# Expert rows of a mixture-of-experts layer: the first one of a token written with its residual, the second added

## The reference

```python
gp = softmax(x @ w_group_router + b_group_router)        # x = rms_norm(h); 4 groups
g_val, g_idx = top_k(gp, 1)
el_sel = expert logits of that group                     # 8 experts each, 32 in all
e_val, e_idx = top_k(softmax(el_sel), 2)
gate = g_val * e_val / sum(e_val)
for e in range(32):
    hdn = silu(x @ w_gate[e]) * (x @ w_up[e])            # 1024 -> 256
    y = y + combine[:, e:e + 1] * (hdn @ w_down[e])      # 256 -> 1024
out = h + y
```

## Time and profile before

| | |
|---|---|
| median of 3 runs | 608.5 us (605.67 to 611.92) |
| the profiled execution | 608.44 us, of which its span is 606.7 us |
| TensorE busy | 536.3 us, 88% |
| DVE, ACT, GpSimd busy | 218.0, 168.9, 139.8 us |
| data moved by DMA | 140.97 MB, 232 GB/s over the span |
| links of the chain that are DMA | 36% of the span |

### The profile page before, as it was taken

How to read it: one execution, slowest core, us unless ns; L and a number is a source line. 1 busy time by engine, 2 the same in 40 slices (tenths; PEclk the granted TensorE clock), 3 DMA queues, 4 the chain that set the end, 5 groups by cost and what they waited for, 6 DMA issues and landing times.

```text
span 606.7 us, 9491 instructions
## 1 busy us (share of the span) xinstructions
PE 536.3 (88%) x3304; PEld 393.1 (65%) x3305; DVE 218.0 (36%) x602; ACT 168.9 (28%) x421; POOL 139.8 (23%) x230
## 2 busy tenths in 40 slices
PE   4899999999989999999978888878987699897794
PEld 4888988987557677788867545555644456554451
DVE  4754234333657755427772112202111112211111
ACT  6743343332434333125431201202111012111010
POOL 0232232222503300004535022222211222222212
PEclk9999999999989999999987999999998979998978
DMA  8741000012312111199979689999999999999993
GB/s 339 269 116 36 19 18 1 19 51 77 111 63 97 42 36 36 35 357 421 398 263 303 223 264 368 361 365 378 360 372 384 411 393 375 375 354 382 372 392 56
DMA packets 33458, 140.97 MB, mean 232 GB/s; under 512 B 10489, under 2 KB 11148, under 8 KB 21351
## 3 DMA queue, kind: packets, MB, share of 16 engines
q1 hardware_dynamic: 25776, 124.33, 53.6%
q0 software_dynamic: 5856, 12.60, 8.7%
q10 hardware_dynamic: 1766, 3.25, 1.4%
HBM read 131.15 MB, written 16.46 MB: 243 GB/s over the span
## 4 chain that ended last, share of the span: by engine, by line
DMA 36%; PE 16%; DVE 2%; issue 2%; ACT 1%; POOL 0%; SPq 0%; ACTq 0%; DVEq 0%; POOLq 0%
DMA expert_w<-in_w_gate 17%; DMA expert_w<-in_w_up 17%; PE ps L884 5%; PE ps L900 2%; DMA token_gates<-gate_rows 2%; PE ps L795 2%; PE ps L521 1%; PE ps L522 1%; PE ps L526 1%; PE ps L780 1%; PE ps L823 1%; PE ps L769 1%; PE ps L912 1%; POOL out L1708 0%; PE ps L871 0%
## 5 line engine op out<-in xcount | busy, mean ns | idle before, releaser
L884 PE MATMUL ps<-expert_w,xT 128*64 128x256 f32 x1120 | 128.5, 387 | 15.2 <-issue 5.6
L884 PEld LDWEIGHTS ps<-expert_w,xT 128*64 128x64 f32 x1120 | 93.7, 140 | 53.4 <-issue 23.5
L900 PE MATMUL ps<-expert_w,hT 128*64 128x512 f32 x272 | 66.6, 633 | 17.2 <-DVE hT L1546 16.0
L1702 POOL DMA_INDIRECT out<-y_sb,idx_now x17 | 27.2, 1597 | 161.2 <-issue 85.2
L1539 DVE SCALAR_TENSOR_TENSOR hid<-s_act,gate,ps 128x256 f32<-128x256 f32 x18 | 12.0, 665 | 140.1 <-ACT s_act L1171 140.1
L900 PEld LDWEIGHTS ps<-expert_w,hT 128*64 128x64 f32 x272 | 22.5, 145 | 50.7 <-issue 48.5
L1171 ACT ACTIVATE s_act<-ps,gate 128x256 f32<-128x256 f32 x18 | 8.5, 473 | 132.1 <-PE ps L884 132.1
L521 PE MATMUL ps<-w_in_hi,aT_hi 128*128 128x384 f32 (+2 forms) x120 | 43.7, 369 | 0.0
L522 PE MATMUL ps<-w_in_lo,aT_hi 128*128 128x384 f32 (+2 forms) x120 | 40.8, 345 | 0.0
L1551 DVE COPY y_sb<-ps 128x512 f32<-128x512 f32 x18 | 12.4, 692 | 76.3 <-PE ps L900 70.8
L1176 ACT ACTIVATE y_sb<-ps 128x512 f32<-128x512 f32 x18 | 10.7, 597 | 80.0 <-PE ps L900 74.6
(11 more groups left out here) (229 smaller groups left out, 944.1 us busy)
## 6 DMA issues: line engine op xcount, KB each, us to landing
expert_w<-in_w_up SPq DMA_DIRECT2D x32, 1024.0 KB, 10.0
expert_w<-in_w_gate SPq DMA_DIRECT2D x30, 1024.0 KB, 9.3
expert_w<-in_w_down SPq DMA_DIRECT2D x30, 1024.0 KB, 9.6
w_in_raw<-in_w_in SPq DMA_DIRECT2D x8, 608.0 KB, 8.6
w_out_raw<-in_w_out SPq DMA_DIRECT2D x8, 512.0 KB, 4.1
token_rows<-h_sb ACTq DMA_DIRECT2D x6, 512.0 KB
out<-h_sb SPq DMA_DIRECT2D x6, 512.0 KB, 11.3
x_sb<-in_x_prompt SPq DMA_DIRECT2D x4, 512.0 KB, 10.7
```

Source lines behind the costliest of these rows:

```text
L884: mm = pe.matmul(ps[r, GU_BANK[q.o], g * FH:(g + 1) * FH], xT[:, q.o, k, r], w_gu(j, b, lane, k, g), start=(k == 0), stop=(k == KD - 1))
L900: mm = pe.matmul(ps[r, 4 + half, :], hT[:, q.o, k, r], w_dn(b, lane, k, half), start=(k == 0), stop=(k == 1))
L1702: pool.indirect_dma_start(out=out, out_offset=bass.IndirectOffsetOnAxis(ap=idx, axis=0), in_=y_sb[:, buf, :], in_offset=None, compute_op=A ...
```

## The change

A token's two experts lie in one group, hence in one lane, so the one with the lower number is always worked on in an earlier pair. The list of slots gets a third factor, "first", 1 where the slot's expert is the lower of the token's two. The row of `out` is no longer prepared: with the first expert's row the gathered row of h is added on DVE (`y_rows`) and the sum is written plainly; only the second expert's row is added by DMA. GpSimd issues both for every pair, with index lists in which the rows of the other kind are out of bounds (`put_rows`). `store_h` and the zeros leave SP's queue. The last pair (experts 15 and 31 are never first) is added in halves as before. The new tables stand in the region of the expert loop's buffers.

```diff
 # SP
-            def store_h(i):
-                sp.wait_ge(h_done, 2 * (i + 1))
-                sp.dma_start(out[i * P:(i + 1) * P, :], h_sb[:, i, :]).then_inc(h_stored, 16)
             load_pair(sp, 0, 0)
-            store_h(0)
-            load_pair(sp, 1, 1, range(3))
-            store_h(1)
-            load_pair(sp, 1, 1, range(3, 6))
-            for i in range(2, NT - 1):
-                store_h(i)
+            load_pair(sp, 1, 1)
             sp.wait_ge(o_mm, 2 * NT)
-            store_h(NT - 1)
 # TensorE
-                slot_product(i, 0, 0, slice(0, 3), False).then_inc(slot_mm, 1)
+                slot_product(i, 0, 0, slice(0, 4), False).then_inc(slot_mm, 1)
...
-                slot_product(NT - 1, 0, 0, slice(1, 3), True).then_inc(slot_mm, 1)
+                slot_product(NT - 1, 0, 0, slice(1, 4), True).then_inc(slot_mm, 1)
...
-                slot_product(i, 128, 1, slice(0, 3), i == NT - 1).then_inc(more_mm, 1)
+                slot_product(i, 128, 1, slice(0, 4), i == NT - 1).then_inc(more_mm, 1)
 # ACT, slot_gates
                 for c in range(2):
-                    ins = act.activation(slot_b[:, i % SLOT_BUFS, c, 1, :], R[:, 224 + E * c:224 + E * (c + 1)], ACT.Copy,
-                                         scale=R[:, 410 + c:411 + c])
+                    for n, at in ((1, 410), (3, 412)):
+                        ins = act.activation(slot_b[:, i % SLOT_BUFS, c, n, :], R[:, 224 + E * c:224 + E * (c + 1)], ACT.Copy,
+                                             scale=R[:, at + c:at + c + 1])
 # ACT, pair: only the last pair is copied by ACT
                 if not last:
                     x_copy(main, j + 1)
-                y_copy(main, j, b)
-                rest_passes(todo, closing, again)
+                else:
+                    y_copy(j, b)
+                rest_passes(todo, lambda n: None, opening)
 # DVE, route_weights
+                dve.tensor_tensor(R[:, 412:413], R[:, 182:183], R[:, 183:184], ALU.is_lt)
+                dve.tensor_tensor(R[:, 413:414], R[:, 183:184], R[:, 182:183], ALU.is_lt)
 # DVE, end of routing
+            def put_rows(idx, factors, put):
+
+                first = factors[:, :, 2]
+                dve.scalar_tensor_tensor(out=put[:, :, 1], in0=first, scalar=2.0 * NO_TOKEN, in1=idx[:, 0:PAIRS], op0=ALU.mult, op1=ALU.add)
+                link("route", route_step, dve.tensor_scalar(put[:, :, 0], first, -2.0 * NO_TOKEN, 2.0 * NO_TOKEN, ALU.mult, ALU.add))
+                dve.tensor_tensor(put[:, :, 0], put[:, :, 0], idx[:, 0:PAIRS], ALU.add).then_inc(idx_done, 1)
+
             dve.wait_ge(idx_done, 13)
+            put_rows(idx_all, gate_all, put_all)
+            put_rows(idx_more, more_all, put_more)
 # DVE, the copy out of PSUM
-            def y_copy(q, n, buf, last=False):
-                dve.wait_ge(q.y_mm, n + 2 if last else n + 1)
+            def y_rows(q, n, buf, rows, g):
+
+                dve.wait_ge(q.y_mm, n + 1)
                 y_free(dve, q, n)
-                dve.tensor_copy(y_sb[:, buf, 512:1024], ps[:, 5, :]).then_inc(q.y_dve, 1)
+                dve.scalar_tensor_tensor(out=y_sb[:, buf, :].rearrange("t (n f) -> t n f", n=2), in0=rows.rearrange("t (n f) -> t n f", n=2),
+                                         scalar=gate[:, g, 2:3], in1=ps[:, 4:6, :], op0=ALU.mult, op1=ALU.add).then_inc(q.y_dve, 1)
 # GpSimd, gate_row
+                step(pool.tensor_scalar(R[:, 352:352 + E], R[:, 256:256 + E], R[:, 413:414], None, ALU.mult))
+                step(pool.tensor_scalar(R[:, 288:288 + E], R[:, 224:224 + E], R[:, 412:413], None, ALU.mult))
+                step(pool.tensor_tensor(R[:, 352:352 + E], R[:, 352:352 + E], R[:, 288:288 + E], ALU.add))
+                step(pool.tensor_tensor(gate_rows[:, i % 2, :, 2], R[:, 352:352 + PAIRS], R[:, 352 + PAIRS:352 + E], ALU.add))
 # GpSimd, the writes
-            pool.wait_ge(h_stored, 16 * NT)
...
-            def add_rows(q, n, buf, idx):
-                pool.indirect_dma_start(out=out, out_offset=bass.IndirectOffsetOnAxis(ap=idx, axis=0),
+            def put_rows(q, buf, g):
+                pool.indirect_dma_start(out=out, out_offset=bass.IndirectOffsetOnAxis(ap=idx_put[:, g, 0:1], axis=0),
+                                        in_=y_sb[:, buf, :], in_offset=None,
+                                        bounds_check=T - 1, oob_is_err=False).then_inc(q.added, 16)
+                pool.indirect_dma_start(out=out, out_offset=bass.IndirectOffsetOnAxis(ap=idx_put[:, g, 1:2], axis=0),
                                         in_=y_sb[:, buf, :], in_offset=None, compute_op=ALU.add,
                                         bounds_check=T - 1, oob_is_err=False).then_inc(q.added, 16)
...
             def more_add(j, n):
-                halves = 1 if isinstance(j, int) and j == PAIRS - 1 else 0
-                ready((over.y_act, n + 1), (over.y_dve, n + 1), (main.added, 16 * (j + 1 + halves)))
-                add_rows(over, n, 3, idx_now[:, 6:7])
-                pool.wait_ge(over.added, 16 * (n + 1))
+                ready((put_set, n + 1), (over.y_dve, n + 1), (main.added, 32 * (j + 1)))
+                put_rows(over, 3, 3)
+                pool.wait_ge(over.added, 32 * (n + 1))
...
-                        pool.wait_ge(main.x_tr, j)
+                        pool.wait_ge(main.y_dve, j)
                     gather_pair(j + 2, (b + 2) % 3, 2 * j + 1)
...
-            pool.wait_ge(idx_done, 9)
+            pool.wait_ge(idx_done, 15)
+            pool.memset(more_gate[:, :, :], 0.0)
             first_more_gather(0)
```

More of the change, by code:

```diff
@@ L288, in pe_y_free @@
                 return
-            pe.wait_ge(main.y_act, j)
             pe.wait_ge(main.y_dve, j)
@@ L324, in y_free @@
         def y_free(eng, q, n):
-            if q is over:
-                if not (isinstance(n, int) and n == 0):
-                    eng.wait_ge(over.added, 16 * n)
-            elif not (isinstance(n, int) and n < 3):
-                eng.wait_ge(main.added, 16 * (n - 2))
+            if q is main and not (isinstance(n, int) and n < 3):
+                eng.wait_ge(main.added, 32 * (n - 2))
         def pT_copy(eng, m, u):
@@ L927, in closing @@
                     hidden_transposes(over, n)
-                    pe.wait_ge(main.y_act, j + 1)
+                    if last:
+                        pe.wait_ge(main.y_act, 1)
                     pe.wait_ge(main.y_dve, j + 1)
                     down(over, b, n)
-                    pe.wait_ge(over.y_act, n + 1)
                     pe.wait_ge(over.y_dve, n + 1)
@@ L1171, in silu, with y_copy @@
                 act.activation(s_act[:, q.o, :], ps[:, GU_BANK[q.o], 0:FH], ACT.Silu, scale=gate[:, g, 1:2]).then_inc(q.silu_done, 1)
-            def y_copy(q, n, buf):
-                act.wait_ge(q.y_mm, n + 1)
-                y_free(act, q, n)
-                act.activation(y_sb[:, buf, 0:512], ps[:, 4, :], ACT.Copy).then_inc(q.y_act, 1)
+            def y_copy(n, buf):
+                act.wait_ge(main.y_mm, n + 1)
+                y_free(act, main, n)
+                act.activation(y_sb[:, buf, 0:512], ps[:, 4, :], ACT.Copy).then_inc(main.y_act, 1)
             first_pass, rest_passes = passes_counter(act)
@@ L1185, in opening @@
                     silu(over, n, 3)
-                def closing(n):
-                    y_copy(over, n, 3)
-                def again(n):
-                    opening(n)
-                    closing(n)
                 todo = first_pass(j, opening)
@@ L1563, in closing @@
                     hT_copy(over, n)
-                    y_copy(over, n, 3)
+                    y_rows(over, n, 3, more_rows, 3)
                 def again(n):
@@ L1575, in pair @@
                 hT_copy(main, j)
-                y_copy(main, j, b, last)
+                if last:
+                    y_copy(j, b)
+                else:
+                    y_rows(main, j, b, g_rows[:, b, :], b)
                 rest_passes(todo, closing, again)
@@ L1760, in pair @@
                         first_more_gather(j + 1)
-                    set_idx(3 + b, j)
+                    pool.tensor_copy(idx_put[:, b:b + 1, :], put_all[:, bass.ds(j, 1), :]).then_inc(idx_set, 1)
                 if last:
-                    ready((idx_done, 13), (main.y_act, j + 1), (main.added, 16 * j))
+                    ready((idx_done, 15), (main.y_act, 1), (main.added, 32 * j))
                     add_half(0, b)
@@ L1767, in pair @@
                 else:
-                    waits = [(idx_set, add_count(j)), (main.y_act, j + 1), (main.y_dve, j + 1)]
+                    waits = [(idx_set, 2 * j + 2), (main.y_dve, j + 1)]
                     if not (isinstance(j, int) and j == 0):
-                        waits.append((main.added, 16 * j))
+                        waits.append((main.added, 32 * j))
                     ready(*waits)
-                    add_rows(main, j, b, idx_now[:, 3 + b:4 + b])
+                    put_rows(main, b, b)
                 with pool.If(todo > 0):
@@ L1800, in _ @@
```

(2 more changed lines are left out.)

51 lines of the change are left out of this document (31 added, 20 removed).

## The result

| | before | after |
|---|---|---|
| median (lowest to highest) | 607.42 us (605.67 to 611.92) | 621.78 us (620.59 to 622.35) |
| ratio, 95% interval | | 1.0222 (1.0162 to 1.0282) |
| span of the profiled execution | 606.7 us | 619.9 us |

The forecast was 606.1 with a range of 600.5 to 612.5, so it missed by 15.7 us. Three views of the kernel after show where the time lies.

What follows compares the result with a forecast made beforehand. The prediction took the DMA engines, full mostly with weights from 361 to 571 us, as the bound. Span 606.7 + 2.3 for a later start − 4.6 for cheaper writes = 604.4, with 1.7 around it 606.1 us; range 600.5 to 612.5.

Steps and rivals of the forecast that it cites:

- What bounds the kernel: Expert loop: the chain is weight loads for 209.4 us from 361.49 to 570.89, with DMA engines full; then compute.
- Part 1: SP's queue: six base stores leave, worth 8.5 us of DMA, but costed at nothing because pair 2's load goes out unchanged.
- Part 2: End of routing, on the chain to 361.49: grows by 1.2 us, from 0.7 to 4.0.
- The columns: End of routing: slot products with 128 columns in place of 96 take 0.5 us more, from nothing to 2.1.
- ACT's two blocks: End of routing: ACT writes two more blocks of slot_b before the last product, about 0.43 us more.
- Part 3: Copy out of PSUM: one DVE operation takes 1.27 us, 0.57 more; two on pair 0's chain make 1.15 us.
- Part 4: Loop: plain writes in place of additions save 6.0 us, added DMAs cost 1.4; the stretch shrinks by 4.6, from 2.0 to 5.9.
- Part 5: GpSimd's queue: pair 0's next gather goes out 4 to 6 us later, but TensorE's limit isn't reached, so no cost.
- the limit: Pair 2's down product, needed for SP to issue pair 5's down weights: TensorE was 7 us ahead there.
- Rival D: GpSimd's queue takes the place of DMA: landing grows by 4 us a pass, TensorE and SP wait, 610.7 us; chance 0.05.
- The sum: Whole kernel: span 606.7 + 2.3 − 4.6 = 604.4 us, with 1.7 around the span 606.1.

Runs made afterwards that it cites:

- e16: e9 with the base stores of h back in SP's queue and GpSimd's wait for them: 606.38 us, ratio 0.9989 to the kernel before.
- e19: The kernel of e16 run once more, on one chip with e18: 606.93 us, ratio 0.9935 to the kernel before.
- e11: e9 with the plain writes made additions, so both DMAs add: 609.79 us, ratio 1.0038 to the kernel before.
- e9: e1 with GpSimd's gather for pair j + 3 issued ahead of pair j's second pass: 600.96 us, ratio 0.9897 to the kernel before.
- e12: e9 with all rows in the plain write and none added: 599.08 us, ratio 0.9878 to the kernel before.
- e1: The changed kernel with GpSimd's loop head moved to the start of a block of instructions: 608.31 us, ratio 1.0026 to the kernel before.
- e6: e1 with all rows in the plain write and none added: 607.44 us, ratio 1.0007 to the kernel before.
- e2: The changed kernel without GpSimd's code for third and later passes: 609.79 us, ratio 1.0040 to the kernel before.
- e3: The kernel before with dead code and 13 tiny operations added on GpSimd, its loop 312 instructions long: 615.92 us, ratio 1.0168.
- e13: e1 with ACT's stores of the gates counted on two semaphores in turn: 608.44 us, ratio 1.0009 to the kernel before.
- e18: The kernel of e9 run once more, on one chip with e19: 603.00 us, ratio 0.9895 to the kernel before.

## Why the prediction failed, step by step

- **What bounds the kernel.** Right for the kernel before, and incomplete. I stopped at the chain, which names only what ended last. Beside the 209 us of DMA ran a second path, GpSimd's queue in pair 6 and TensorE behind it, with 10 us less. The wait of 4.88 at 485.06 was in the trace; I had looked at the one of 1.31.
- **Part 1**, base stores worth nothing: 0 forecast, probably 2 to 5 us (e16, e19), not clear of noise on one chip, cause open.
- **Part 2**, end of routing: +1.2 forecast, +3.0 in the profile after, inside the bounds of 0.7 to 4.0. The columns cost next to nothing (I had 0.5). ACT's two blocks cost the 0.4 that I had. Of the rest 1.5 us are there before the last tile is routed (its copy to h_sb starts at 307.60 after 306.06): that is upstream of all my terms, and ACT's queue behind a store's landing, where TensorE waits 1.2 at 295, wasn't in the sum at all. Another 1.0 is the last stretch, where 40 small products took 4.27 us after 3.28, at a mean granted clock of 0.66 in 315 to 330 after 0.77.
- **Part 3**, DVE's operation: 1.29 us for 1.27, and +1.0 on the path for 1.15. Right.
- **Part 4**, an addition against a write: 6.0 us forecast, 6.0 and 5.8 measured (e11, e9, e12; 7.0 and 6.0 at equal bytes), with 1.02 and 1.58 us of GpSimd to issue them. Right as a price. It is worth its 4.6 us only while DMA bounds, and in e1 and e6 the chain leaves the weights at some 455, after less than half of the stretch of 361 to 571.
- **Part 5**, GpSimd's queue, no cost: this is the step that failed, twice. I counted its DMAs, but not its instructions: 57 more in a loop of 255 brought gaps of 5 us, some 13 us in all (e1, e2; 9.5 by dead code alone, e3). And I followed the queue through pair 0 only, where the limit was 7 us off. In pair 6 two passes of 13.0 and 9.6 us stand ahead of the gather for pair 9, and TensorE came to that pair's second pass 8 us late instead of 2.3. Moving the gather gave back some 7 us (e1 and e13 against e9).
- **Rival D** had the right mechanism and sign, at 0.05. It was priced from the landing growing by 4 us; the landing didn't grow (11.6 and 8.3 in e1; before some 12.3 and 8.1 by the issues behind them). The late start, TensorE's clock and two DMAs to issue in each pass were enough. No rival had the length of the code in it.
- **The sum**, redone with what was measured: 606.1, plus 1.7 for the start, minus 2 to 5 for the stores, is 602.8 to 605.8; e9 and e18, where neither obstacle is left, have 601.0 and 603.0. So between nothing and 5 us of their gain have no named source.

## What to carry to other kernels

Behind the chain that bounds there is a next one: for every queue that an edit lengthens, find the place in the whole loop where its consumer already waits longest, and how many us of its own work lie behind that place. What really passes there up to the end, less that work, is the slack, and here it was 10 us. Then count an edit's instructions too, with those of branches that are never taken, where an engine jumps back in a loop. A load (here the gather) that others wait for belongs ahead of writes that nobody waits for: moving one gather turned a change of +0.3% into −1.0%, with the loop's head aligned in both.

## What the runs showed of the hardware

- GpSimd with a loop of 312 instructions from its 585th on stood twice for 4.4 to 5.1 us at each of two jumps back (after, e3); with the loop's head moved to the start of a block and the same work, never (e1). The instruction queue carried 35 packets in the one case, 26 in the other.
- A write of rows by index takes 1.02 us of GpSimd to issue, the same with addition 1.58 (e9, e11: 1.59). An addition costs the engines 6 to 7 us more than a write for some 2.6 MB of rows, 2.3 to 2.7 us per MB (e11, e9, e12).
- 24 KB of gates in rows of 192 bytes needed 11.4 us from issue to landing on ACT's queue while SP's queue took 87% of the DMA engines' time for weights (e1; in the kernel before 16 KB in rows of 128 bytes: 10.2 us, at 86%).
